# The input projection of a hybrid decoder block by 7 block products in place of 8, with its token operands kept in SBUF

## The reference

```python
D_MODEL = 2048; SEQ = 512; N_META = 16; CHUNK = 64; N_HEADS_A = 8   # head size 128
IN_SIZES = (QK_DIM, QK_DIM, V_DIM, V_DIM, N_HEADS_A, N_HEADS_A, POOL_DIM, D_MODEL, D_MODEL)  # q k v z b a p gates

h = concat([meta_tokens, x])                       # 16 + 512 tokens
hn = rms_norm(h, norm_mix_w)
proj = hn @ w_in                                   # 528 x 2048 times 2048 x 9232
q, k, v, z, b_logit, a_logit, p, gate_a, gate_b = split(proj)
qkv = silu(causal_dwconv(concat([q, k, v]), conv_w))           # 4 taps along the tokens
o = gated_delta_rule_chunked(l2_norm(q), l2_norm(k), v, sigmoid(b_logit), g)
o = rms_norm(o) * o_norm_w * silu(z);  y_a = o @ w_proj_a
pooled = causal_multiscale_pool(p)                 # windows 2, 4, 8, 16, minus p
y_b = (pooled @ pool_w) * pool_scale @ w_proj_b
merged = sigmoid(gate_a) * y_a + sigmoid(gate_b) * y_b
h = h + merged @ w_out
h = h + swiglu_ffn(rms_norm(h, norm_ffn_w));  out = rms_norm(h, norm_final_w)[:, N_META:]
```

## Time and profile before

| | us |
|---|---|
| median of 3 runs | 2724.44 |
| the profiled execution, span of the core | 2722.7 |
| PE busy | 2651.1 (97%) |
| DVE busy | 1835.8 (67%) |
| ACT busy | 998.4 (37%) |
| POOL busy | 341.3 (13%) |
| start to the first product of unit 0 | 31.3 |
| q, k, v | to 330 |
| gates and delta rule | to 860 |
| p, z | to 1054 |
| merge and output projection | to 1400 |
| feed-forward | to the end |

### The profile page before, as it was taken

One profiled execution on the slowest core, in us unless ns is written; L12 is line 12 of the kernel. 1 busy time (PEld: TensorE's weight loads), 2 busy tenths in 40 slices (PEclk: granted clock), 3 DMA queues, 4 the chain that ended last, 5 costly groups with the idle time before them and its releaser, 6 DMA issues.

```text
span 2722.7 us, 44448 instructions
## 1 busy us (share of the span) xinstructions
PE 2651.1 (97%) x17640; PEld 2422.1 (89%) x17640; DVE 1835.8 (67%) x1771; ACT 998.4 (37%) x1025; POOL 341.3 (13%) x350
## 2 busy tenths in 40 slices
PE   8999999999999999998989999999999998999997
PEld 8999988888889987887879999999999996888885
DVE  4444555555553234558888888888888887888886
ACT  4443322222222242223354444444444543333333
POOL 5000044444442420110000000000000000000000
PEclk9999999999999999999999999999999999999998
DMA  4333222223223433778425444545445449756661
GB/s 139 98 92 92 79 78 78 77 77 85 77 77 93 108 93 122 254 241 306 165 97 170 155 150 146 177 152 161 154 154 177 146 141 316 227 194 214 220 213 62
DMA packets 345654, 398.73 MB, mean 146 GB/s; under 512 B 11481, under 2 KB 300386, under 8 KB 344418
## 3 DMA queue, kind: packets, MB, share of 16 engines
q1 hardware_dynamic: 286514, 334.34, 39.1%
q10 hardware_dynamic: 59072, 63.44, 6.8%
HBM read 325.92 MB, written 71.83 MB: 146 GB/s over the span
## 4 chain that ended last, share of the span: by engine, by line
PE 92%; DVE 3%; issue 2%; DMA 1%; ACT 1%; POOL 0%; SPq 0%; DVEq 0%; ACTq 0%; POOLq 0%
PE psum L1973 34%; PE psum L2285 10%; PE psum L2283 10%; PE psum L2284 10%; PE psum L2260 6%; PE psum L2261 6%; PE psum L2262 6%; PE psum L2133 2%; PE psum L2128 1%; PE psum L1922 1%; PE psum L1950 1%; DMA w_raw<-in_w_proj_a 1%; PE psum L2112 1%; PE psum L2205 1%; DVE hq L1630 0%
## 5 line engine op out<-in xcount | busy, mean ns | idle before, releaser
L1973 PE MATMUL psum<-hn_hi,w_hi 128*128 128x264 f32 (+1 forms) x1600 | 450.4, 330 | 0.0
L1973 PE MATMUL psum<-hn_hi,w_lo 128*128 128x264 f32 (+1 forms) x1600 | 449.6, 330 | 0.0
L1973 PE MATMUL psum<-hn_lo,w_hi 128*128 128x264 f32 (+1 forms) x1600 | 449.4, 330 | 0.0
L1296 DVE TENSOR_TENSOR w_lo<-w_raw,w_hi 128x1024 fp32r<-128x1024 f32 x144 | 186.9, 1299 | 253.8 <-ACT w_hi L892 253.4
L1973 PEld LDWEIGHTS psum<-hn_lo,w_hi 128*128 128x128 f32 x1600 | 269.0, 188 | 22.7 <-issue 0.7
L1973 PEld LDWEIGHTS psum<-hn_hi,w_lo 128*128 128x128 f32 x1600 | 268.6, 188 | 22.5
L1973 PEld LDWEIGHTS psum<-hn_hi,w_hi 128*128 128x128 f32 x1600 | 269.0, 188 | 22.0 <-issue 0.2
L892 ACT ACTIVATE w_hi<-w_raw 128x1024 fp32r<-128x1024 f32 x144 | 152.0, 1057 | 371.9 <-PE psum L1973 345.5
L2260 PE MATMUL psum<-dn_hi,act_hl 128*128 128x512 f32 x616 | 242.3, 393 | 15.8 <-DVE hq L1630 14.6
L2261 PE MATMUL psum<-dn_lo,act_hl 128*128 128x512 f32 x616 | 241.5, 392 | 0.0
L2262 PE MATMUL psum<-dn_hi,act_hl 128*128 128x512 f32 x616 | 241.3, 392 | 0.0
(11 more groups left out here) (352 smaller groups left out, 6318.1 us busy)
## 6 DMA issues: line engine op xcount, KB each, us to landing
w_raw<-in_w_in SPq DMA_DIRECT2D x144, 512.0 KB, 3.9
ffn_raw<-in_w_ffn_gate SPq DMA_DIRECT2D x44, 1024.0 KB, 6.4
ffn_raw<-in_w_ffn_up SPq DMA_DIRECT2D x44, 1024.0 KB, 6.5
dn_raw<-in_w_ffn_down SPq DMA_DIRECT2D x40, 1024.0 KB, 7.3
act_hl<-act_dram SPq DMA_DIRECT2D x70, 512.0 KB, 9.3
act_dram<-comb_hi ACTq DMA_DIRECT2D x22, 896.0 KB, 4.2
act_dram<-comb_lo ACTq DMA_DIRECT2D x22, 896.0 KB, 6.2
out_raw<-in_w_out SPq DMA_DIRECT2D x16, 1024.0 KB, 9.7
```

The lines of the kernel that those rows point to most:

```text
L1296: dve.tensor_tensor(wlo[s][:], raw[s][:], whi[s][:].bitcast(F32), ALU.subtract).then_inc(S["lo_ready"], 1)
L1973: ins = pe.matmul(o, lhs, r, start=kt == 0 and i == 0, stop=kt == 4 * n_chunks - 1 and i == 2)
```

## The change

The whole product `hn @ w_in` is made in Strassen's form as Winograd wrote it. The 528 tokens are cut into two halves of 264 (256 real and 8 meta tokens), the 2048 rows of the weights into two of 1024, and the 256 columns of a unit into two of 128. Four sums of the token blocks (`operand_sums`) are made once, so seven token operands, each split into high and low, stay in SBUF. They take the place of `hn_hi`, `hn_lo` and of `qkv`; q, k, v, the pooled means and silu(z) are therefore stored to DRAM and read back, and so are the delta rule's outputs o.

Per unit, the weights come as two loads of 1 MB in all into one of two buffers. VectorE forms two pair sums in one operation of 2048 (`pair_sums`), and `two` and `four` sums of 1024 are made by GpSimd, or by VectorE where a half of the delta rule ends. The seven blocks are split as seven pieces of 1024 on ScalarE and VectorE. TensorE runs seven products of 8 x 3 matmuls with 264 moving columns (k, v, p, q) or 256 (z, gates). Three PSUM banks take them; ScalarE copies a bank out when its partial sum is whole (`evict`), and VectorE adds or subtracts the next (`combine`).

The order of the units is now k, v, p, q, z (20 units written out, `N_FIRST`), then the gates beside the delta rule, then the merge. In the gates stage `PIECE` is 14 matmuls of 256 in place of 8 of 512; what the other engines do for a product stands behind the step in which the product ends (`ended_in`). For the convolution ScalarE now makes the first tap and VectorE three. The pooled product stands directly ahead of the merge, and the gating of o is done there for four column blocks over all heads.

```diff
@@ constants @@
-BODY_CHUNKS = N_GATES * 4 // CH
-PIECE = 24 * BODY_CHUNKS // (2 * STEPS)
+PRODUCTS = 7
+BODY = N_GATES // CH
+PIECE = BODY * PRODUCTS * 24 // (2 * STEPS)
+def ended_in(step):
+    return [p for p in range(PRODUCTS * BODY) if -(-24 * (p + 1) // PIECE) - 1 == step]
@@ TensorE @@
+            def unit_products(x, begins=False):
+                a, b, c = x.banks()
+                width = WIDE if x.wide() else QTR
+                for q in range(PRODUCTS):
+                    pe.wait_ge(S["lo_ready"], x.item(q) + 1)
...
+                    out = PS[:, (a, b, a, c, a, c, a)[q], 0:width]
+                    s_hi_q, s_lo_q = sx_hi[OPERAND_OF[q]], sx_lo[OPERAND_OF[q]]
+                    start, stop = q in (0, 1, 3), q in (1, 5, 6)
+                    for k in range(HEADS):
+                        hi, lo = w_in_hi[x.ring(q)][:, k, :], low_of(x, q)[:, k, :]
+                        for j, (w, t) in enumerate(((hi, s_hi_q), (hi, s_lo_q), (lo, s_hi_q))):
+                            ins = pe.matmul(out, w, t[:, k, 0:width], start=start and k == 0 and j == 0,
...
             def gate_products(n):
-                for u in range(BODY_CHUNKS // 4):
-                    for c in range(4):
-                        yield from chunk_products(G_GATES + BODY_CHUNKS * n + 4 * u + c, c, c, 4, hn_real,
...
+                for i in range(BODY):
+                    yield from unit_products(gate_unit(n, i))
@@ before the merge @@
-            with pe.Fori(0, N_Z - 1) as u:
-                z_unit(u)
+            pe.wait_ge(S["c_ready"], 3 * N_IN)
...
                 ins.then_inc(S["zb_done"], 1)
-            z_unit(N_Z - 1)
...
+                pe.wait_ge(S["z_lo"], CH)
@@ VectorE @@
+            def unit_event(x, ahead, q, sums=False):
+                a, b, c = x.banks()
+                if q == 0:
+                    weight_low(x, 2)
+                    weight_low(x, 3)
+                elif q == 1:
+                    dve.wait_ge(S["chunk_used"], x.item(1) + 1)
+                    combine(x, b, 0, 0, "sum", 3 * x.u + 1)
+                    weight_low(x, 4)
+                elif q == 2:
+                    weight_low(x, 5)
+                elif q == 3:
+                    weight_low(x, 6)
+                elif q == 4:
+                    dve.wait_ge(S["chunk_used"], x.item(4) + 1)
+                    combine(x, a, 1, 1, "place", 3 * x.u + 3)
+                    if ahead is not None:
+                        pair_sums(ahead)
+                elif q == 5:
+                    if ahead is not None:
+                        weight_low(ahead, 0)
+                        weight_low(ahead, 1)
+                    dve.wait_ge(S["chunk_used"], x.item(5) + 1)
+                    combine(x, c, 1, 0, "bank", 3 * x.u + 2)
+                    if ahead is not None and sums:
+                        sum_two(ahead)
+                        sum_four(ahead)
...
+                    for k in range(STEPS):
+                        next(steps_of_half)
+                        for p in ended_in(STEPS * hf + k):
+                            i, q = p // PRODUCTS, p % PRODUCTS
+                            unit_event(gate_unit(n, i), following(n, i, final), q, i % 2 == 1)
@@ ScalarE, behind the gates @@
             act.wait_ge(S["gates_stored"], FREE["gates_stored"] + 16 * N_GATES)
...
+            for n in range(CH):
+                merge_high(n)
+            for i in range(CH):
+                gated_high(i)
+                zb_high(i)
@@ SyncE: the delta rule's rows for the next half, and the reloads for the merge @@
+                    sp.wait_ge(S["vn_product"], v)
+                for b, t0 in ((7, QT), (8, K_T), (6, VT)):
+                    sp.dma_start(B[b][:], qkv_dram[t0 + h0:t0 + h0 + GH, :, tok].rearrange("h p t -> p h t")) \
+                        .then_inc(S["staged_rows"], 16)
...
+            sp.wait_ge(S["chunk_used"], final_unit + 1)
+            saved_all(N_FIRST)
+            sp.dma_start(pooled[:, :, :], pooled_dram.rearrange("h p t -> p h t")).then_inc(S["meta_landed"], 16)
...
+            sp.wait_ge(S["o_saved"], FREE["o_saved"] + 16 * 2 * CH)
+            o_load(CH - 1)
```

1208 lines of the change are left out of this document (756 added, 452 removed).

## The result

The changed kernel takes 2796.67 us (2793.19 to 2797.55, 4 runs) against 2724.42 us before, a ratio of 1.0265 with a 95% interval of [1.0251, 1.0280]. It is 72 us slower; the forecast was 2685 us, 39 us faster. The profiled execution has a span of 2794.5 us.

What follows compares the result with a forecast made beforehand. TensorE, with 92% of the chain of waits, was taken to bound the kernel: 2722.7 - 89.0 + 3 + 24 + 11 + 12 = 2683.7 us of span, 1.7 more for the median: 2685 us; eight-in-ten range 2650 to 2718 us.

Steps and rivals of the forecast that it cites:

- the cover in VectorE's queue: In wide units and beside the delta rule, VectorE's new weight work stays mostly hidden from TensorE: +3 and +24 us.
- What the products give back (-89): Seven block products per unit shorten TensorE's work: 43.2 us in fifteen wide units, 45.8 in twenty narrow, together 89.0.
- Wide stage (+3, bounds 0 and 15): In the projection's convolved and pool units, VectorE's queue and GpSimd's added sums cost 3 us in all, between 0 and 15.
- rival C: VectorE bounds the fifteen wide units through GpSimd's sums, 2.2 us each instead of 0.2: 2715 us; chance 13%.
- 0.8 of the 1.7 goes that way: In a convolved unit, GpSimd's sums take 0.8 us of the 1.7 us by which VectorE's split is early for TensorE.
- The gates stage (+24, bounds 8 and 48): Beside the delta rule, TensorE waits on VectorE's queue 3 us per half, 8 x 3 = 24 us; per-half bounds 1 and 6.
- Followed through one half, most events fit; two don't: Beside the delta rule, only two VectorE queue events delay its steps: about 2 us at a half's start, 1 us in step 3.
- rival B: Beside the delta rule its chain becomes the bound, 10 us exposed per half, and the kernel is slower: 2741 us; chance 12%.
- The start (+11): Up to the end of the first unit with logits: first product at 47.6 us, end at 80.4 against 69.2; bounds +5, +16.
- The handover (+12): Between last gate product and merge: 10 us of late splits of o, 2 us of low clock; bounds 6 and 20.
- Everything behind the merge: The stretch after the merge was to stay as before, with no change in time.
- The clock: TensorE falls to its lower clock level in the gap before the merge, costing 2 us; counted nowhere else.

Runs made afterwards that it cites:

- the first run: The changed kernel with the sums of two and of four of units 1 to 20 on VectorE instead of GpSimd: 2766.80 us, ratio to before 1.0164.

## Why the prediction was wrong

The terms for the products, the start and the handover came out. What failed is one step, the cover in VectorE's queue: how far the new weight work is hidden from TensorE, in the wide units and above all in the gates stage.

**What the products give back (-89): right.** A wide unit without waits takes (313.62 - 151.22) / 8 = 20.30 us, not 20.19: 1.7 us over fifteen units. Beside the delta rule two steps without a wait take 773.58 - 768.48 = 5.10 us in the changed kernel, the 2.55 each of the forecast, so the 117 ns for 256 columns held for the sixteen gate units. For the z units, among which other work stands, it can't be read as cleanly.

**Wide stage (+3, bounds 0 and 15): wrong by 40.0, 33.0 of it for GpSimd's sums, in rival C's place.** The slack was right: 1.7 us until TensorE would ask. The delay was not: "0.8 of the 1.7 goes that way" was read from a split of 1.22 us that became 1.99. What that split met stands just ahead of those rows, and neither they nor the prediction show it:

```profile
477.68 1.28 POOL L816 TENSOR_TENSOR gdn<-gdn,strict 128x512 f32<-128x512 f32 x1 [0.94 <-DVE gdn L1480]
```

GpSimd was in this operation until 478.96 us when the split was due at 478.05. The split stood still for most of these 0.9 us and ran its 1.22 after them; the two masks of the earlier trace rows in turn took 3.02 us beside it in place of 2 x 1.04. So 0.77 us was the rest of an operation that had begun before, not a share of the block. The new sum is 2.40 us long and begins with the splits (180.26 and 180.28): 4.59 - 2.35 = 2.24 us of delay, 1.7 of it covered, 0.55 left, which is the 0.55 us of the trace. The rule of the Trainium skill that the prediction put aside (SBUF — State Buffer, "Who interferes with whom": such a pair excludes each other for the whole instruction) is what these rows show. Rival C's 2.2 us per unit had the delay right and forgot the cover; that its 15 x 2.2 = 33 us is what the first run measured is luck. The dearer part was not in the wide units' rhythm: 7.76 us in unit 1, where the prediction didn't look at what stands ahead of the sum in GpSimd's queue, and the units beside the pool windows and the meta state, up to 24.5 and 24.2 us (20.4 and 22.2 with the sums on VectorE). The first run puts all of it at 33.0 us; of the 7.0 that stay, 4.4 are its three waits.

**The gates stage (+24, bounds 8 and 48): the step that failed, by 67.7.** VectorE's load was right: 106 us per chunk, 425.37 measured for four. "Followed through one half, most events fit; two don't" was wrong. It counted lengths without GpSimd and looked for what delays the delta rule. But TensorE waits most for the weight work itself: 38.6 of some 65 us for a block product's last combination, which stands behind a pair sum of 3.25 and splits of 4.99 us, against 15.8 us for operations of the delta rule. In place of 3 us per half the stage loses 3 + 67.7 / 8 = 11.5, above rival B's 7.9 at which the sign turns. That B's 10 us lies near is partly luck: B charged ten events ahead of the delta rule's results and had its place at the half's turn, where the wait is 1.54 us; the 4.06 us stand in the middle of each half, where GpSimd makes the sums. The chunk takes 143 to 147 us, over the 138 that was to mean B.

By the runs, 16 us of the 67.7 are GpSimd's sums with the order of the combination (each edit alone gets all of them back), 46 go with the rest of the weight work, at most 17 of them as meetings with GpSimd's masks, and 6 remain. That split is against a forecast with 24 us of waits in it: thin weight work takes the stage no lower, because 25.8 us of other waits stay. Two of those the prediction had at nothing: the wait at the stage's opening, 6.0 us in the changed kernel and 3.4 before, and the turns of TensorE's loop, 8.8 us in three. The 1.86 us ahead of the pooled product, which the bounds put here, belong to the handover.

**The start (+11): 3.5 us short.** 48 us for the first product was right; unit 0 and the logits took 36 us and not 33. **The handover (+12): right.** The waits around the pooled product are 1.86, 0.76, 1.61 and 5.31 us and the merge starts at 1123.21, 8.5 us more than its cover; the rest, 3.9, is a wait of 1.26 in the merge and, it seems, the low clock. **Everything behind the merge: right,** -0.9. **The unrolled code at nothing: right there,** at 20.30 us a unit.

**The clock: a term that the sum has at the handover but not in the gates stage.** TensorE's busy time there should have fallen by the products' 36.6 us, from 526.6 to 490; it is 520.4, 30 us more. A granted clock of 0.96 over 586 us is worth up to 23 of them; the rest stays open. When VectorE's weight work is thinned, it is 495.95 us at 0.99. So close to half of the miss of this stage isn't idle time but a slower TensorE, and most of it goes when the waits go. After 4.06 us of idle the next 14 matmuls take 710.63 - 707.61 = 3.02 us, after the wait of 1.54 at 739.56 they take 1.75. The length of the stop alone doesn't decide it: behind two waits of 1.39 us, at 685.61 and at 758.21, the granted clock is 0.75 once and 1.00 once. Where it is under 1.00, part of the stretch is at the lower of the two levels, 1.2 GHz (the granted clock is the last number but two):

```profile
707.00:717.00 10.00, 9.39 (x67) 9.39 (x68) 4.57 (x9) 3.96 (x5) 6.54 (x6) 0.83 0.52 174
685.60:692.40 6.80, 6.79 (x45) 6.80 (x46) 3.66 (x5) 3.14 (x5) 2.26 (x3) 0.75 0.00 0
755.00:765.00 10.00, 8.61 (x75) 8.41 (x74) 7.57 (x9) 3.40 (x6) 6.41 (x5) 1.00 0.01 2
```

## What to carry to other kernels

Fewer matmuls paid for with elementwise work pay only where that work's engine can run ahead. By share of busy time VectorE had room (73% in the gates stage here, 84% in the feed-forward stretch, where TensorE is busy 98%); beside the chain it had none. My reading is that a chain of short steps shares its queue; the runs fit it but don't separate it from the amount of work, since spreading the same work gained nothing and only less work did. So use the cheaper algorithm where the queue is free and the plain one beside the chain: that mix was 75 us under the version with seven products throughout, level with the kernel before, and 7 us under it with half of the logits moved. Part of the 75 us are the sums on VectorE, TensorE's loop written out and the early load. Count the clock too: a wait that lowers it costs more than its length. And when work is given to GpSimd to relieve VectorE, count on VectorE too what is left of its operation wherever the two meet.

## What the runs showed of the hardware

A GpSimd addition of 1024 elements lasts 2.40 us against VectorE's 1.22, and VectorE stands still meanwhile: two splits of 2.35 us took 4.59 beside it. In these rows the engine that comes second waits for the rest of the operation that the other is in, and then runs at its own length. It works both ways: VectorE's pair sum of 768.03 came during a GpSimd operation (767.86) that lasts until 769.13 and took 3.25 us in place of 2.28; the mask behind that operation, 1.04 us alone, then waited for the pair sum and took 3.09. And GpSimd's busy time fell by 57 us when only VectorE's work was thinned. The mask alone, the operation of 767.86, and the mask beside the pair sum of 768.03:

```profile
714.08 1.04 POOL L1005 TENSOR_TENSOR gdn<-levels,small 128x512 f32<-128x512 f32 x1
...
767.86 1.27 POOL L1014 TENSOR_TENSOR gdn<-gdn,keep 128x512 f32<-128x512 f32 x1 [1.88 <-DVE gdn L1933]
769.09 3.09 POOL L1005 TENSOR_TENSOR gdn<-levels,small 128x512 f32<-128x512 f32 x1
```

Edits that each shorten one stage by 16 to 18 us shortened it by 16 us together. A turn of TensorE's loop between two chunks stopped it for 2.1 to 3.3 us in the kernels with 256-column products (the two kernels with this loop written out are 8 and 10 us faster), and for nothing in the kernel before; what sets that one apart wasn't tried. The Trainium skill (Advanced Engine Details and Errata, "Control Flow Timing") gives a branch that is always taken some 51 ns and one that compares some 108. A turn here is dearer by a factor of 19 or more, so it isn't the branch alone; what it is stays open.
